# Two norms between projections, computed per 256 tokens beside the neighbouring projections' matmuls

## The reference

```python
mix = jnp.concatenate([o_f, o_c], axis=-1) @ w_out[l]      # mix_out
x = x + rms_norm(mix, g_mix_post[l])
h = rms_norm(x, g_mem_pre[l])
...                                  # q = h @ w_q (mem_q), attention over 256 memory rows
ca = ... @ w_o                                              # mem_o
x = x + rms_norm(ca, g_mem_post[l])
h = rms_norm(x, g_ffn_pre[l])
x = x + rms_norm(swiglu(h, w_gate_up[l], w_down[l]), g_ffn_post[l])   # ffn_up, ffn_down
```

## Time and profile before

| | us |
|---|---|
| median of 3 runs | 1508.93 (1508.07 to 1509.24) |
| the profiled execution | 1507.83 |
| its span | 1506.0 |
| PE busy | 1480.1 (98%) |
| DVE busy | 817.7 (54%) |
| ACT busy | 583.2 (39%) |
| POOL busy | 237.1 (16%) |

### The profile page before, as it was taken

How to read it: one execution, slowest core, us unless ns; L and a number is a source line. 1 busy time by engine, 2 the same in 40 slices (tenths; PEclk the granted TensorE clock), 3 DMA queues, 4 the chain that set the end, 5 groups by cost and what they waited for, 6 DMA issues and landing times.

```text
span 1506.0 us, 21173 instructions
## 1 busy us (share of the span) xinstructions
PE 1480.1 (98%) x7946; PEld 1207.5 (80%) x7946; DVE 817.7 (54%) x1208; ACT 583.2 (39%) x887; POOL 237.1 (16%) x203
## 2 busy tenths in 40 slices
PE   8999999999998999999999999999999999999998
PEld 6888669877886888888888678888887888888887
DVE  6434673456636434343332786747666776767332
ACT  6223665443244222222323642334764443434231
POOL 0200101042014000000000565545422000000000
PEclk9999999999999999999999999999999999999999
DMA  5523003421021333433232122332203333333321
GB/s 172 196 86 111 30 2 114 139 84 63 23 84 56 87 109 84 111 84 112 84 111 84 56 85 84 95 102 84 58 2 84 101 94 94 101 88 108 112 84 56
DMA packets 152811, 132.24 MB, mean 88 GB/s; under 512 B 6300, under 2 KB 137628, under 8 KB 152740
## 3 DMA queue, kind: packets, MB, share of 16 engines
q1 hardware_dynamic: 150836, 128.11, 27.5%
q0 software_dynamic: 848, 3.17, 0.6%
q10 hardware_dynamic: 1056, 0.00, 0.0%
HBM read 129.15 MB, written 2.12 MB: 87 GB/s over the span
## 4 chain that ended last, share of the span: by engine, by line
PE 91%; DVE 5%; POOL 2%; ACT 1%; issue 1%; DMA 0%; SPq 0%; DVEq 0%; ACTq 0%; POOLq 0%
PE ps L1854 26%; PE ps L1856 26%; PE ps L1855 26%; PE ps L2135 3%; POOL x_t L701 2%; DVE rstd L1767 1%; PE ps L2223 1%; PE ps L2318 1%; PE ps L2239 1%; PE ps L2327 1%; PE ps L457 1%; PE ps L2145 1%; DVE a_lo L1302 1%; PE ps L2063 1%; DVE work L1282 1%
## 5 line engine op out<-in xcount | busy, mean ns | idle before, releaser
L1854 PE MATMUL ps<-a_hi,w_hi 128*128 128x512 f32 (+2 forms) x1656 | 644.8, 389 | 11.1 <-DVE a_lo L1302 6.8
L1856 PE MATMUL ps<-a_hi,w_lo 128*128 128x512 f32 (+2 forms) x1656 | 639.4, 386 | 0.0
L1855 PE MATMUL ps<-a_lo,w_hi 128*128 128x512 f32 (+2 forms) x1656 | 639.0, 386 | 0.0
L1854 PEld LDWEIGHTS ps<-a_hi,w_hi 128*128 128x128 f32 (+1 forms) x1656 | 310.8, 188 | 83.8 <-issue 9.7
L1856 PEld LDWEIGHTS ps<-a_hi,w_lo 128*128 128x128 f32 (+1 forms) x1656 | 310.8, 188 | 64.0
L1855 PEld LDWEIGHTS ps<-a_lo,w_hi 128*128 128x128 f32 (+1 forms) x1656 | 311.0, 188 | 62.3 <-issue 0.7
L780 ACT ACTIVATE w_hi<-raw 128x2048 fp32r<-128x2048 f32 x116 | 221.9, 1913 | 332.6 <-PE ps L1856 330.8
L1241 DVE TENSOR_TENSOR w_lo<-raw,w_hi 128x2048 fp32r<-128x2048 f32 x92 | 210.7, 2290 | 240.0 <-ACT w_hi L780 239.6
L656 POOL TENSOR_TENSOR w_lo<-raw,w_hi 128x2048 fp32r<-128x2048 f32 x26 | 119.8, 4608 | 445.9 <-ACT w_hi L780 418.2
L1689 DVE TENSOR_TENSOR arena<-ps,rstd 128x512 f32<-128x512 f32 x88 | 60.1, 689 | 166.0 <-PE ps L1856 159.7
L1767 DVE RECIPROCAL rstd<-std 128x512 f32<-128x512 f32 x24 | 80.5, 3353 | 26.3 <-ACT std L1141 26.3
(11 more groups left out here) (237 smaller groups left out, 1320.5 us busy)
## 6 DMA issues: line engine op xcount, KB each, us to landing
raw<-in_w_gate_up SPq DMA_DIRECT2D x44, 512.0 KB, 4.6
raw<-in_ffn_w_up SPq DMA_DIRECT2D x44, 512.0 KB, 4.7
raw<-in_attn_w_in SPq DMA_DIRECT2D x36, 512.0 KB, 4.3
raw<-in_w_in SPq DMA_DIRECT2D x24, 512.0 KB, 4.6
raw<-in_w_down SPq DMA_DIRECT2D x22, 512.0 KB, 3.9
raw<-in_ffn_w_down SPq DMA_DIRECT2D x22, 512.0 KB, 4.2
raw<-in_w_mem_kv SPq DMA_DIRECT2D x16, 512.0 KB, 4.4
raw<-in_w_out SPq DMA_DIRECT2D x8, 512.0 KB, 4.0
```

The costliest lines, as they stand in the source:

```text
L1854: pe.matmul(dst, s_hi, m_hi, start=start, stop=False, skip_group_check=across)
L1855: pe.matmul(dst, s_hi, m_lo, start=False, stop=False, skip_group_check=across)
L1856: return pe.matmul(dst, s_lo, m_hi, start=False, stop=stop, skip_group_check=across)
```

## The change

The last two chunks of mix_out and mem_o (four tiles) are computed twice over 256 tokens: all four tiles for the first half of the tokens, then all four for the second (`halved_closing`). The first two chunks of mem_q and ffn_up likewise: both chunks on the first half, then both on the second (`halved_opening`). Sum, root, reciprocal, spread, scaling, addition, `a_hi` and `a_lo` are done per half (`halved_out` on ACT, `halved_residual` on DVE). All additions to the stream are now DVE's, through PSUM bank 6. The two chunks' `w_lo` move from POOL to DVE, between operand tiles. POOL adds squares per half and four tiles of the next norm's squares at the end; DVE reduces the other four. The third chunk of mem_q and ffn_up uses banks 6 and 7. The filler matmuls of these two transitions are gone. The rest of the program is the same.

The core of the diff:

```diff
+        HALVES = slice(0, 256), slice(256, S)
+        HALF_BANKS = (0, 1, 2, 3), (7, 0, 2, 3)
+        STAGED_BANK, FACTOR_BANK = 6, (5, 7)
+        HALVED = {"mix_out": ("mix_post", 0), "mem_o": ("mem_post", 4)}
+        OPENED = {"mem_q": ("mix_out", "mix_post", "mem_pre"), "ffn_up": ("mem_o", "mem_post", "ffn_pre")}
+        def third(ch):
+            return ch.gemm.name in OPENED and isinstance(ch.i, int) and ch.c == 2
...
+                pool.wait_ge(norm.sq, 1)
+                pool.tensor_copy(square_sum, squares[:, 0, :]).then_inc(norm.added, 1)
+                for k in range(1, 4):
+                    add_square(norm, k + 1, k, slice(0, S))
+                for t in range(3):
+                    add_square(norm, t + 5, t, HALVES[0])
+                for t in range(3):
+                    add_square(norm, t + 9, t, HALVES[1])
+            def sum_last_four(name, pre):
+                pool.wait_ge(norms[pre].ready, 2 * KT)
+                pool.wait_ge(norms[pre].sq, KT)
+                of = x_squares[pre]
+                for n in range(3):
+                    pool.wait_ge(x_added[name], 2 * KT + n)
+                    pool.tensor_tensor(of[:, 4, :], of[:, 4, :], of[:, 5 + n, :], ALU.add).then_inc(x_added[name], 1)
...
-            for name, y, gemm in (("mix_post", y_1, "mem_q"), ("mem_post", y_1, "ffn_up")):
+            for _, name, pre in OPENED.values():
                 sum_squares(norms[name])
-                split_lo(Chunk(G[gemm], 0, 2, 0))
-                add_residual(name, y)
-                split_lo(Chunk(G[gemm], 0, 2, 1))
+                sum_last_four(name, pre)
...
+                def half_tile(h, t):
+                    if h == 0:
+                        act.wait_ge(half_done, base + t + 1)
+                        act.wait_ge(norm.added, CREDIT + t + 1)
...
+                split_hi(chs[0])
+                tile(0), tile(1)
+                split_hi(chs[1])
+                tile(2)
+                split_hi(chs[2])
+                tile(3)
+                for t in range(4):
+                    half_tile(0, t)
+                root(0)
+                half_tile(1, 0)
+                hi(0, 0), hi(0, 1)
+                split_hi(chs[3])
+                half_tile(1, 1)
+                hi(0, 2), hi(0, 3)
+                half_tile(1, 2)
+                hi(0, 4)
+                half_tile(1, 3)
+                hi(0, 5)
+                split_hi(Chunk(G[following], 0, 2, 0))
+                hi(0, 6)
+                root(1)
+                hi(0, 7)
+                for k in range(KT):
+                    hi(1, k)
+                    squared(pre, k)
...
+                def chain(h):
+                    of = slice(2 * h, 2 * h + 2)
+                    dve.wait_ge(norm.std, h + 1)
+                    dve.reciprocal(tok_rstd[:, of], tok_std[:, of]).then_inc(norm.inverse, 1)
+                    dve.wait_ge(norm.inverse, 2 * h + 1)
+                    dve.tensor_tensor(diagonal[:, HALVES[h]].rearrange("p (b n) -> p b n", b=2),
+                                      ident[:, :].rearrange("p (b n) -> p b n", b=1).to_broadcast([128, 2, 128]),
+                                      tok_rstd[:, of].rearrange("p (b n) -> p b n", n=1).to_broadcast([128, 2, 128]),
+                                      ALU.mult).then_inc(norm.inverse, 1)
+                def scale_and_add(h, k):
+                    n, x = h * KT + k, x_t[:, k, HALVES[h]]
+                    staged = ps[:, STAGED_BANK, k % 2 * 256:k % 2 * 256 + 256]
+                    if n >= 2:
+                        dve.wait_ge(x_added[name], n - 1)
+                    dve.tensor_tensor(staged, y[:, k, HALVES[h]], ps[:, FACTOR_BANK[h], 0:256], ALU.mult)\
+                       .then_inc(norm.value, 1)
+                    dve.wait_ge(norm.value, n + 1)
+                    dve.tensor_tensor(x, staged, x, ALU.add).then_inc(x_added[name], 1)
+                def lo(h, k):
+                    dve.wait_ge(pre.hi, h * KT + k + 1)
+                    dve.scalar_tensor_tensor(out=a_lo[:, k, HALVES[h]], in0=x_t[:, k, HALVES[h]], scalar=vcol(after, k),
+                                             in1=a_hi[:, k, HALVES[h]].bitcast(F), op0=ALU.mult, op1=ALU.subtract)\
+                       .then_inc(pre.ready, 1)
+                chain(0)
+                for h in range(2):
+                    dve.wait_ge(norm.spread, h + 1)
+                    scale_and_add(h, 0)
+                    for k in range(KT):
+                        if k + 1 < KT:
+                            scale_and_add(h, k + 1)
+                        elif h == 0:
+                            chain(1)
+                        if h == 0 and k == 2:
+                            split_here(Chunk(G[gemm], 0, 2, 3))
+                        lo(h, k)
+                    if h == 0:
+                        split_here(Chunk(G[following], 0, 2, 0))
+                half_sum(after)
+                dve.wait_ge(pre.added, 1)
+                dve.wait_ge(x_added[name], 2 * KT + 3)
+                dve.tensor_tensor(square_sum, part_sum, x_squares[after][:, 4, :], ALU.add).then_inc(pre.added, 1)
+                split_here(Chunk(G[following], 0, 2, 1))
+                invert(pre)
...
+            def half_sums(norm, h, part):
+                def by_half(of, first, last):
+                    for b in (2 * h, 2 * h + 1):
+                        at = pe.matmul(ps[:, 4, b:b + 1], of[:, b * 128:(b + 1) * 128], ones[:, 0:1],
+                                       start=first and b == 2 * h, stop=last, skip_group_check=True)
+                    return at
+                if part == 0:
+                    pe.wait_ge(norm.added, CREDIT + (10 if h else 7))
+                    if h:
+                        pe.wait_ge(norm.std, 1)
+                    by_half(square_sum, True, False)
+                else:
+                    pe.wait_ge(norm.sq, 12 if h else 8)
+                    by_half(squares[:, 3, :], False, True).then_inc(norm.sum, 1)
+            def half_spread(norm, h):
+                pe.wait_ge(norm.inverse, 2 * h + 2)
+                pe.matmul(ps[:, FACTOR_BANK[h], 0:256], ones[:, :], diagonal[:, HALVES[h]], start=True, stop=True)\
+                  .then_inc(norm.spread, 1)
+            def halved_closing(gemm):
+                name, base = HALVED[gemm]
+                norm = norms[name]
+                for h in range(2):
+                    for t in range(4):
+                        ch, j = Chunk(G[gemm], 0, 2, 2 + t // 2), t % 2
+                        if h == 0:
+                            chunk_ready(ch)
+                            pe.wait_ge(freed["act"], ch.freed + (j + 1))
+                        elif t:
+                            pe.wait_ge(half_left, base + (1, 3, 4)[t - 1])
+                        whi, wlo = weights(ch.slot, KT)
+                        cols = slice(j * 128, j * 128 + 128)
+                        for k in range(KT):
+                            last = three(ps[:, HALF_BANKS[h][t], 0:256], (whi[:, k, cols], wlo[:, k, cols]),
+                                         (a_hi[:, k, HALVES[h]], a_lo[:, k, HALVES[h]]), k == 0, k == KT - 1)
+                            if h == 1 and t == 0 and k == 2:
+                                half_sums(norm, 0, 0), half_sums(norm, 0, 1)
+                            if h == 1 and t == 0 and k == 6:
+                                half_spread(norm, 0)
+                        last.then_inc(tile_done if h else half_done, 1)
+            def halved_opening(gemm):
+                of, name, pre = OPENED[gemm]
+                chs, left = [Chunk(G[gemm], 0, 2, c) for c in range(2)], CREDIT + G[of].freed_end
+                for h in range(2):
+                    for ch in chs:
+                        if h == 0:
+                            chunk_ready(ch)
+                        whi, wlo = weights(ch.slot, KT)
+                        for k in range(KT):
+                            if ch.c == 0:
+                                pe.wait_ge(norms[pre].ready, h * KT + k + 1)
+                            for j in range(2):
+                                if h == 0 and k == 0:
+                                    pe.wait_ge(freed["act"], left - 2 if ch.c == 0 else left - 1 + j)
+                                cols = slice(j * 128, j * 128 + 128)
+                                last = three(ps[:, 2 * ch.c + j, HALVES[h]], (whi[:, k, cols], wlo[:, k, cols]),
+                                             (a_hi[:, k, HALVES[h]], a_lo[:, k, HALVES[h]]), k == 0, k == KT - 1, across=True)
+                                if h == 1 and k == KT - 1:
+                                    last.then_inc(tile_done, 1)
+                            if h == 0 and ch.c == 0 and k in (1, 2):
+                                half_sums(norms[name], 1, k - 1)
+                            if h == 0 and ch.c == 0 and k == 6:
+                                half_spread(norms[name], 1)
```

(8 more changed lines are left out.)

120 lines of the change are left out of this document (66 added, 54 removed).

## The result

| | before | after |
|---|---|---|
| median, us | 1508.53 (1508.07 to 1509.24) | **1494.8** (1494.51 to 1495.27) |
| span of the profiled execution | 1506.0 | 1493.0 |
| first transition | 59.07 | 51.90 |
| second transition | 59.07 | 52.2 |

The account below looks back on a forecast made before the run. PE, busy 98%, bounds the kernel. Per transition, own work 50.2 us, waits 0.8 and 0.4, and POOL's 0.6 gave about 52.2 against 59.1; 6.8 taken twice, 13.6 less: 1495.3 us, range 1490.5 to 1502.0.

Parts of the forecast that it names:

- PE's own work: Per transition: 384 matmuls of 256 tokens (46.1 us), sums (2.4) and spreads (1.7), 50.2 us together.
- DVE's step: One 256-token step on DVE (scale, add, make a_lo): taken as 1.20 us, bounds 1.0 and 2.0.
- rival 3: Half-width DVE instructions cost as much as whole ones, 2.0 us a step: slower, 1517.5 us; chance 0.07.
- Rival 1: DVE steps 0.1 us longer, or the clock falls after the new waits: gain 7.6, time 1501.3 us; chance 0.21.
- The DVE queue's times: From third chunk's start: first `w_lo` starts 20.9 us, second ends 32.3; PE reaches next projection's second chunk at 31.5.
- The two new waits: PE waits 0.8 us before the next projection's second chunk and 0.4 us before the following norm's sum.
- The allowance for POOL: 0.6 us per transition for POOL's adds of squares slowing DVE's `w_lo`; bounds 0 and 2.1.
- What is removed: Per transition, the 9.6 us gap before the next projection's first matmul and 2.9 us of slow opening in its first chunk.
- The clock: PE's granted clock was forecast to be 1.0 in the transitions after the change.
- The total: 52.2 us per transition against 59.1, 6.9 less; 6.8 taken twice, a gain of 13.6 us.
- Rival 2: PE never waits, DVE at 1.0 us a step: gain 17.8, time 1491.1 us; chance 0.08.
- Rival 4: First half's norm chain held until the second half is done, so the 9.6 us gap stays: 1510.3 us; chance 0.03.

Follow-up runs that it names:

- the longer step: The kernel after with one more 128 x 256 scaling on DVE in each of a passage's 16 steps: 1507.54 us (ratio 0.9995).
- The short `w_lo`: The kernel after with DVE's `w_lo` of the next projection's first and second chunks formed for only 256 of 2048 columns: 1491.93 us (ratio 0.9892).
- the version two additions ahead: The kernel after with DVE's first half two additions ahead of its low parts instead of one, ACT's high parts reordered to match: 1492.32 us (ratio 0.9895).

## Why the prediction was right

**PE's own work**, 50.2 us, measured 50.53 where nothing stops PE, 0.3 more. The 256-token spacing is 0.120, the first sum 0.81 (312.64 to 313.45), the half spread 0.42 (314.97 to 315.51 less one spacing, taken 0.43). Part of the 0.3 is the sums: counted to the second matmul behind it (313.65, less one spacing) a sum costs 0.89 and not 0.81. With the 262 and 518 cycles of the Trainium skill ("TensorE: Matmul & The Clock Gate", Back-to-back issue gap), halving would cost 0.5 in place of 2.6 us and the 50.2 would be an estimated 48.1; this trace does not agree with them here either.

**DVE's step**, taken as 1.20 between 1.0 and 2.0, is 1.20. This was the number on which rivals 1 to 3 turned, and the longer step shows how steeply: at 1.65 the gain is gone. The point from which rival 3 would decide was put at 1.7 a step; at 1.65 the time of the kernel before was reached. Rival 1's price for a longer step, 14 steps all visible, would make 6.4 us a transition of 0.46 more; the two intervals grew by 5.97 and 5.63, since the first half had idle time to give.

**The DVE queue's times**, from the start of the third chunk (300.05): the first `w_lo` at 20.9, measured 20.8; the second one's end at 32.3, measured 32.3; PE at that chunk at 31.5, measured 31.4. The parts are a little off and cancel: the wait for ACT behind it is 0.40 where 0.65 was taken, and the `a_lo` right behind the first `w_lo` is 0.96 where 0.4 was.

**The two new waits** were found where they were put, with the releasers named: before the second chunk, 0.8 taken, 1.0 measured; before the following norm's sum, 0.4 taken, 0.28 and 0.64 measured. The short `w_lo` shows that the first is DVE's queue, and the second too in the first transition; in the second transition 0.39 of it is something else, behind POOL's adds, which the prediction did not have.

**The allowance for POOL**, 0.6 with the bounds 0 and 2.1, is the one term with the wrong reason. Without it the times gave 51.6, and 51.9 and 52.2 were measured, so 0.3 to 0.6 was wanted. But 0.3 of that is PE's own work (50.53 for 50.2), and the rest the wait before the sum. That the allowance came out near is luck. I had POOL's adds slowing DVE; in the trace it is mostly DVE that holds POOL: two adds of squares take 3.46 us beside DVE's `w_lo`, and DVE loses 0.5 us once, on that `a_lo` at 323.05.

**What is removed.** The prediction counted 2.9 us of slow opening beside the clock of 0.88, and rival 1 charged 1.7 us for a stretch at that clock. The runs show the opening at the pace of DVE and POOL, and no difference between 0.88 and 1.00 in it (30.62 and 30.61 from sum to sum). The 2.9 us were there to be removed, but rival 1 took its price for the clock from a stretch in which the clock cost nothing. What a fall would cost in the transitions of the kernel after no run shows, since none stood there.

**The clock** stayed at 1.0, as the forecast had it and rival 1 had not. **The total**: 14.0 us from the two transitions (13.6 taken, after rounding 6.9 down to 6.8), less 1.0 elsewhere that no step of mine names. So the total agrees better than its parts, and that is luck too.

Rival 2, no wait, is refuted by the rows of the kernel after and nearly reached by the version two additions ahead (1492.3; the rival gave 1491.1). Rival 4 is refuted by the sum of the first half at 312.64, with no wait before it, while the second half's matmuls go on behind it.

## What to carry to other kernels

When a norm between two projections leaves the matmul engine waiting, halve the tokens on both sides: the price is the shorter matmuls' overhead and one more sum and spread (50.5 us of PE's own work here, where the 512-token matmuls alone took 43.5), and the gain is the wait for the chain. Then the elementwise queue is the next bound, and each of its steps counts in full: look for its idle time behind other engines before adding anything to it, and let it run two operations ahead where it waits. Before a large elementwise operation is moved to a free engine, ask whether that engine stops the busy one: here it cost half the gain. And before filler is put in to hold the clock, look at what ends the stretch behind it: where it is another engine, as in the transitions of the kernel before, a lower clock costs nothing; where it is PE itself, as in the third norm (below), it costs.
